# A router's chain in a two-block transformer kernel: a low part given to GpSimd, ranks first on VectorE, and a weight granule split later

## The reference

```python
z = rms_norm_2(h, norm_ffn[i])
...
logits = (xt @ w_router).astype(jnp.float32)
top_logit, top_idx = lax.top_k(logits, TOP_K)        # 2 of 8 experts
gates = jax.nn.softmax(top_logit, axis=-1)
...                                                   # rows sorted by expert, blocks of 128
xs = xt_pad[tok_buf].reshape(n_blocks, EXPERT_BLOCK, D)
ys = lax.map(expert_block, (xs, block_expert))        # swiglu with that expert's weights
out = jnp.zeros((T + 1, D), ys.dtype).at[tok_buf].add(ys * gate)[:T]
```

## Time and profile before

| | us |
|---|---|
| median of 3 runs | 1756.12 (1755.95 to 1757.22) |
| the profiled execution's own time | 1756.61 |
| its span, first to last instruction | 1754.5 |
| TensorE matmul busy | 1716.2 (98%) |
| VectorE busy | 1322.1 (75%) |
| ScalarE busy | 1137.8 (65%) |
| GpSimd busy | 71.9 (4%) |
| first expert matmul | 773.33 |

### The profile page before, as it was taken

One profiled execution on the slowest core, in us unless ns is written; L12 is line 12 of the kernel. 1 busy time (PEld: TensorE's weight loads), 2 busy tenths in 40 slices (PEclk: granted clock), 3 DMA queues, 4 the chain that ended last, 5 costly groups with the idle time before them and its releaser, 6 DMA issues.

```text
span 1754.5 us, 23799 instructions
## 1 busy us (share of the span) xinstructions
PE 1716.2 (98%) x8856; PEld 1422.6 (81%) x8856; DVE 1322.1 (75%) x1178; ACT 1137.8 (65%) x1178; POOL 71.9 (4%) x80
## 2 busy tenths in 40 slices
PE   7999999899999999999999999999999999999999
PEld 6799998887788886678888888888888888888887
DVE  5765444675555467678898898898998988988987
ACT  5555553665544367757777777777777777777775
POOL 2200000220100000020000000000000000000000
PEclk9999999999999999999999999999999999999999
DMA  9445553644655554149999999999999999999995
GB/s 361 152 168 193 188 184 91 216 144 147 203 185 192 168 174 132 38 142 362 367 361 371 370 335 363 366 366 364 352 347 378 367 365 369 328 368 371 360 370 212
DMA packets 227794, 477.72 MB, mean 272 GB/s; under 512 B 11148, under 2 KB 54512, under 8 KB 227688
## 3 DMA queue, kind: packets, MB, share of 16 engines
q1 hardware_dynamic: 220080, 468.30, 74.4%
q10 hardware_dynamic: 7096, 7.42, 1.4%
q0 software_dynamic: 512, 0.54, 0.1%
HBM read 474.36 MB, written 1.08 MB: 271 GB/s over the span
## 4 chain that ended last, share of the span: by engine, by line
PE 75%; DVE 2%; ACT 2%; issue 1%; DMA 0%; ACTq 0%; DVEq 0%; POOLq 0%; POOL 0%
PE bank L693 23%; PE bank L696 23%; PE bank L694 23%; PE bank L1169 2%; PE bank L1334 1%; PE bank L687 1%; PE bank L1292 1%; DVE w_lo L1988 1%; ACT w_hi L1430 0%; ACT e L1512 0%; PE bank L1301 0%; PE bank L1300 0%; PE bank L851 0%; PE bank L838 0%; DMA gain_b<-in_norm_ffn 0%
## 5 line engine op out<-in xcount | busy, mean ns | idle before, releaser
L2516 DVE TENSOR_TENSOR w_lo<-raw,w_hi 128x2048 fp32r<-128x2048 f32 x333 | 757.5, 2289 | 105.9 <-ACT w_hi L1903 102.7
L1903 ACT ACTIVATE w_hi<-raw 128x2048 fp32r<-128x2048 f32 x333 | 633.8, 1919 | 175.2 <-PE bank L696 175.2
L1988 DVE TENSOR_TENSOR w_lo<-raw,w_hi 128x2048 fp32r<-128x2048 f32 (+3 forms) x117 | 253.4, 2173 | 157.6 <-ACT w_hi L1430 157.5
L693 PE MATMUL bank<-w_hi,xg_hi 128*128 128x512 f32 x896 | 353.7, 395 | 0.4 <-DVE xg_lo L2482 0.4
L696 PE MATMUL bank<-w_hi,xg_lo 128*128 128x512 f32 x896 | 349.6, 390 | 0.0
L694 PE MATMUL bank<-w_lo,xg_hi 128*128 128x512 f32 x896 | 349.0, 389 | 0.0
L1430 ACT ACTIVATE w_hi<-raw 128x2048 fp32r<-128x2048 f32 (+3 forms) x117 | 210.6, 1809 | 114.1 <-PE bank L696 86.7
L693 PE MATMUL bank<-w_hi,a_hi 128*128 128x512 f32 (+3 forms) x544 | 211.3, 388 | 10.6 <-DVE w_lo L1988 5.9
L696 PE MATMUL bank<-w_hi,a_lo 128*128 128x512 f32 (+3 forms) x544 | 204.8, 376 | 0.0
L694 PE MATMUL bank<-w_lo,a_hi 128*128 128x512 f32 (+3 forms) x544 | 204.6, 376 | 0.0
L696 PEld LDWEIGHTS bank<-w_hi,xg_lo 128*128 128x128 f32 x896 | 168.2, 188 | 35.8
(11 more groups left out here) (263 smaller groups left out, 1978.4 us busy)
## 6 DMA issues: line engine op xcount, KB each, us to landing
raw<-in_moe_w_gate SPq DMA_DIRECT2D x112, 1024.0 KB, 7.0
raw<-in_moe_w_up SPq DMA_DIRECT2D x112, 1024.0 KB, 7.3
raw<-in_moe_w_down SPq DMA_DIRECT2D x112, 1024.0 KB, 6.6
raw<-in_w_mlp SPq DMA_DIRECT2D x32, 1024.0 KB, 5.3
raw<-in_ffn_w_gate SPq DMA_DIRECT2D x22, 512.0 KB, 3.9
raw<-in_ffn_w_up SPq DMA_DIRECT2D x22, 512.0 KB, 4.8
raw<-in_ffn_w_down SPq DMA_DIRECT2D x11, 1024.0 KB, 4.8
raw<-in_w_in SPq DMA_DIRECT2D x9, 1024.0 KB, 12.5
```

Source lines behind the costliest of these rows:

```text
L693: pe.matmul(o, hi, h, start=start, stop=False)
L1903: act.activation(w_hi[:, g % NSPLIT, :], raw_at(g, GRAN), ACT.Copy).then_inc(hi_made, 1)
L1988: dve.tensor_tensor(w_lo[:, g % NSPLIT, 0:n], raw_at(g, n), w_hi[:, g % NSPLIT, 0:n].bitcast(F32), ALU.subtract).then_inc(lo_made, 1)
L2516: dve.tensor_tensor(w_lo[:, g % NSPLIT, :], raw_at(g, GRAN), w_hi[:, g % NSPLIT, :].bitcast(F32), ALU.subtract).then_inc(lo_made, 1)
```

## The change

GpSimd makes the low part of z for the second half of the tokens, in two steps: zrow times rstd into gain_b (its content is not needed any more), then that minus z_hi. VectorE makes only the first half's, so that rank and pick follow one operation earlier. On ScalarE and on VectorE the split of the third granule moves behind the four xg_hi and the four xg_lo. The other instructions are the same.

```diff
@@ GpSimd
             norm(NFFN1)
 
+            pool.wait_ge(rstd_made, NFFN1 + 1)
+            chained(pool.tensor_scalar(gain_b[:], zrow[:, 1, :], rstd[:, NFFN1, 1:2], None, ALU.mult))
+            pool.wait_ge(zhi_made, NB)
+            pool.tensor_tensor(z_lo[:, 1, :], gain_b[:], z_hi[:, 1, :].bitcast(F32), ALU.subtract).then_inc(zlo_made, 1)
             for half in range(2):
@@ ScalarE
                 act.activation(z_hi[:, b, :], zrow[:, b, :], ACT.Copy, scale=rstd[:, NFFN1, b:b + 1]).then_inc(zhi_made, 1)
-            hi_to(NG + 2)
             act.wait_ge(gap_made, 1)
             act.activation(gate[:, 1, :], gate[:, 0, :], ACT.Exp).then_inc(g_exp, 1)
...
                 xg_hi_out(k, bank[6 + (TM + k) % 2])
+            hi_to(NG + 2)
@@ VectorE
-            dve.wait_ge(zhi_made, NB)
-            for b in range(NB):
-                dve.scalar_tensor_tensor(z_lo[:, b, :], zrow[:, b, :], rstd[:, NFFN1, b:b + 1], z_hi[:, b, :].bitcast(F32),
-                                         ALU.mult, ALU.subtract).then_inc(zlo_made, 1)
+            dve.wait_ge(zhi_made, 1)
+            dve.scalar_tensor_tensor(z_lo[:, 0, :], zrow[:, 0, :], rstd[:, NFFN1, 0:1], z_hi[:, 0, :].bitcast(F32),
+                                     ALU.mult, ALU.subtract).then_inc(zlo_made, 1)
             dve.wait_ge(rk_psum, 1)
...
             dve.tensor_scalar(n_items[:], count[:, 1:2], 2.0, float(N_EXPERTS), ALU.mult, ALU.add).then_inc(items_made, 1)
-            lo_to(NG + 2)
...
                 xg_lo_out(k, bank[6 + (TM + k) % 2])
+            lo_to(NG + 2)
             dve.wait_ge(g_exp, 1)
```

## The result

The changed kernel took 1760.77 us (median of 22 runs, 1755.54 to 1763.24), the kernel before beside it 1757.5 (22 runs, 1755.04 to 1759.8): a ratio of 1.0019 [1.0012, 1.0025], 3.3 us slower. Between the means it is 2.9 us (standard error 0.6). The forecast was +0.2 us, 1756.3, at most 1758.2. The change stays, just, within the 0.2% that the forecast took for no change; its sum and its range do not hold. Against the 1757.5 that before takes here the forecast would read 1757.7 and its upper end 1759.6, and the result still lies above it. The profiled execution took 1761.73 (span 1759.6, before 1754.5).

The account below looks back on a forecast made before the run. TensorE's own work was taken to bound the kernel from the first expert matmul on. The hold's +0.84 us less the granule's 0.66 gave +0.2, 1756.3 us on the median's scale; range 1753.9 to 1758.2.

Parts of the forecast that it names:

- The granule's move: VectorE, ahead of the first xg_lo: the third granule's low part leaves the chain, -0.66 us, no cost in the loop.
- the case in dispute, 16 columns: VectorE's small chosen: held by GpSimd's subtraction (+0.2 us in sum) or slipping through (-0.2, chance 0.15).
- The hold: GpSimd's subtraction keeps VectorE's chosen out until about 763.96, so rank comes at 765.51, 0.84 us later.
- the product's price: GpSimd's product of 1024 columns, zrow times rstd: taken as 1.4 us, between bounds of 0.9 and 2.5.
- the rival of the slow first pass: GpSimd's product takes 2.5 us, holding the cast, its subtraction the one-hot rows: +1.2 us, 1757.3; chance 0.13.
- The granted clock falls: TensorE idles 1.9 us before the ranks and its clock drops: 1.7 us lost, 1758.0 with the hold; chance 0.07.
- the forecast's own case: GpSimd's subtraction, from 761.63, holds chosen on VectorE; with the granule's gain +0.2 us, 1756.3; chance 0.45.
- the memsets: GpSimd's later memsets holding VectorE's 0/1 matrices: value 0, upper bound one memset, 0.5 us.

Follow-up runs that it names:

- x1: Kernel before with only the third granule's split moved behind the four xg_hi and xg_lo; 1755.95 us against 1757.55, ratio 0.9996.
- x6: Changed kernel without GpSimd's product, so half of the low part is wrong; 1760.54 us, ratio 1.0021 to the kernel before.
- x5: Changed kernel with GpSimd's product waiting until chosen is there; 1762.69 us, ratio 1.0029 to the kernel before.
- x2: Changed kernel with 34 instead of 16 filling matmuls ahead of TensorE's wait for chosen; 1757.49 us against 1757.55 before, ratio 1.0007.
- x3: Kernel before without the 16 filling matmuls ahead of TensorE's wait for chosen; 1757.88 us, ratio 1.0003.
- x4: Kernel before with only GpSimd's half of the change, the granule left where it was; 1761.11 us, ratio 1.0024.
- x9: Changed kernel with 4 instead of 13 filling matmuls between the ranks and the first gather; 1761.75 us, ratio 1.0023 to the kernel before.
- x10: Changed kernel with GpSimd's product written as two tensors, rstd at step zero; 1758.19 us, ratio 1.0010 to the kernel before.
- x11: Changed kernel run again unchanged, on the same chip as its 34-filling-matmul version; 1759.05 us, ratio 1.0014 to the kernel before.
- x12: Changed kernel with 34 instead of 16 filling matmuls, run again beside the changed kernel; 1759.87 us, ratio 1.0012 to the kernel before.
- x7: Kernel before with the granule moved and VectorE making z_lo's second half after rank and pick, without GpSimd; 1755.84 us against 1757.29, ratio 0.9993.

## Why the prediction was wrong

**Right.** TensorE bounds the loop, and whatever happens to the first expert matmul goes one for one into the end. The granule's move gains 0.66 (0.74 in x1) and costs nothing in the loop. A VectorE operation can be kept out until a GpSimd operation ends, small ones too: the case in dispute, 16 columns, took 2.36 us instead of 0.18. The hold ends 0.15 to 0.2 us before GpSimd's recorded end, if one takes the plain duration off, as in the earlier trace rows. The Trainium skill (SBUF — State Buffer, Who interferes with whom) states for two SBUF inputs that the second to issue blocks fully, whatever the size; the trace agrees down to 16 columns. The same section says it of VectorE's two-port mode beside any GpSimd operation, and the one-input operations held in x1 and x6 agree with that. It is no rule for every small operation: the cast of after and the four pick of x5 ran free while the product was under way.

**First failed step: the product's price.** "Bounds: 0.9 us ... and 2.5 us ... I take 1.4 us, nearer the lower end because one input is read." It took 2.86, above both bounds. The lower bound came from memsets, which read nothing, and the number of inputs turned out to be no measure: the form with two inputs of step 1 takes 2.34 for the same columns, the form with a step of 0 takes 1.89, and the one with a value per partition is the slowest. The Trainium skill's GPSIMD Engine Reference (Elementwise — side-by-side cycle accounting) gives the best case from which 1.5 us was an estimate; no form here came down to that. So it was the rival of the slow first pass that occurred, priced at +1.2 with a chance of 0.13; x2 shows +1.12. That the two are so close is partly luck, since the details differ: the rival had the product hold the cast and the subtraction the one-hot rows, while in after and x2 the cast ran free and the four one-hot rows were held to the product's end, then chosen through the subtraction, and in x2 rank's second operation by a memset, which makes 0.36 of the 1.12.

**Second failed step: the clock.** "The granted clock falls (0.07)", priced at 1.7 lost at most. I had seen the 1.9 us of idle and had one row where such an idle was followed by a fall and one where it was not. With the longer hold the idle became 2.58 us. The slow ranks or slow filling stand in the profiles of after, x3, x4, x6, x9, x10 and x11, which have 2.1 to 4.2 us of idle there, and not in those of x2 and x12, which have 0.47. It cost 2.35 us in after's profile and 0.96 in x11's; on average over the runs it is not settled (1.5 +- 0.5 over all, 0.2 +- 0.6 side by side). Two rows with opposite outcomes should have given something near even chances, not 0.07: the second of them, where the 2.6 us of idle are a sum and the longest stretch is 2.18, lies where the clock fell in 9 of 13 profiles. And the price was taken from TensorE's own lost time, while here the ranks had lost the z_lo that used to lie beside them (x3).

The range failed with these two steps together. They stood as separate rivals, each inside it, although a slower product makes a longer hold and so a longer idle. Their own prices added, 1.2 and 1.7, give 1756.1 + 2.9 = 1759.0, above the 1758.2 of the range.

**Third: which operations are caught.** The sum holds chosen alone, from 761.63 on. But by the earlier trace rows the four one-hot rows run until 761.88, and they are of the same form, one tensor and one value per partition, as the held scaling of the earlier trace rows; the prediction speaks of two inputs. So the forecast's own case did not exist: with a shorter product the subtraction starts earlier and catches the fourth one-hot row (4.52 us in x6, 2.33 in x10). And the memsets: "Value 0, upper bound one memset, 0.5." A cast took 0.26 longer beside one memset in x1, rank's second operation 0.36 in x2, and x6's row was kept out through five of them. The same five cost nothing in after: chosen was let go between the subtraction and the first memset, and z_lo, with two tensor inputs, took its 1.28 beside them (766.12).

The sum by what was measured: hold +1.70 up to the first gather (x2), less 0.58 behind it for the granule, is +1.12; with 1.5 for the fall it is +2.6, against +2.9 between the means and +3.3 between the medians of the first comparison. As the 1.5 comes largely from that same comparison, this is no independent proof. What stays open is in how many executions the clock falls, and so its exact share.

## What to carry to other kernels

Work given to GpSimd beside a chain of small VectorE operations can cost the chain up to GpSimd's whole duration; some operations pass, and which one is caught changes with the moment (x5, x6, x10). Reordering on the same engine, with TensorE taking last what is made last, gave the same earlier rank at a cost of 0.2 us (x7); that its time is less than before's the runs do not yet show by themselves. And a hold is priced together with the idle that it makes on TensorE: ask what the matmuls behind that idle cost at half the clock, and whether anything still lies beside them.

## What the runs showed of the hardware

- GpSimd, 128x1024 float32: 2.86 us for a product with a value per partition, 2.34 for two tensor inputs, 1.89 with the second input at step 0.
- The hold works both ways. A product of 2.86 us lasted 4.01 when VectorE's z_lo was under way first (x5). And it can span several GpSimd instructions: a subtraction and the five memsets behind it let one waiting one-hot row in only after 4.5 us (x6). It need not: in x10 the row was let go behind the subtraction.
- A GpSimd operation does not hold every VectorE operation beside it: a cast took its 0.18 and four pick their 0.87 beside the product with a value per partition (after, x5), and z_lo with two tensor inputs its 1.28 beside memsets (after, x2, x10), while a cast (x1, x3) and rank's second operation (x2) were held by a memset.
- Idle of 2.1 to 2.6 us on TensorE, between small matmuls, was followed by several microseconds at 1.2 GHz in the profiles of after, x3, x4, x9, x10 and x11; with 0.47 us of idle in the same place the clock stayed at 2.4 GHz (x2, x12). It is not so in each execution: behind the idle stretch near 745, 2.0 to 2.9 us long, the clock fell in 9 of 13 profiles.
